# A routed encoder layer on one core: router products on rows before their norm, and the last expert's final tiles in five buffers

## The chip, the cores and the metric

The kernel runs on one core of one Trainium2 chip. The metric is the device time of one execution in microseconds. Engines are called PE (TensorE), VectorE (DVE), ScalarE (ACT), GpSimd (POOL) and SP (SyncE); SP, ScalarE and GpSimd also issue DMAs, each from a queue of its own.

## The reference, cut to what matters

One layer (DEPTH is 1) with the pooling mixer, then 16 experts that each choose 258 of the 2064 tokens, then a final norm. Everything is float32.

```python
D_MODEL, SEQ, N_META, N_EXPERTS, D_EXPERT = 1024, 2048, 16, 16, 2048
def _rmsnorm(x, g):
    return x * rsqrt(mean(x * x, axis=-1) + 1e-6) * g
h = concatenate([meta, x])                              # 2064 rows
u = _rmsnorm(h, norm_mix)
h = h + _pool_mixer(u, pool_w, pool_scale)              # window means, then a 256x256 map per group
u = _rmsnorm(h, norm_ffn)
aff = softmax(u @ router_w)                             # over the 16 experts
g, idx = top_k(aff.T, 258)                              # each expert picks its tokens
for e in range(16):
    xs = u[idx[e]]
    ys = (silu(xs @ w_gate[e]) * (xs @ w_up[e])) @ w_down[e] * g[e]
    h[idx[e]] += ys
out = _rmsnorm(h, norm_final)[16:]
```

A row's norm multiplies the whole row by one number and each column by its norm_ffn. So the logits of a row can also be had as (h @ (norm_ffn * router_w)) times that row's inverse root.

## The kernel before, in words

**Phase 1** works through 19 tiles of 128 rows (each shares 16 rows with its neighbour). The engines each run a written-out pipeline, `step(i0, j)`, in which `here(a)` stands for work on tile i0 + a: steps -1 to 2 are written out, 12 run in loops of four, the rest (up to step 21) is written out as the drain. For tile i:

- ScalarE squares the rows and takes the root (L839, L827), VectorE scales the band matrices by the inverse root (`make_band`, L1081), PE multiplies the rows by them (L1537, step i-1), ScalarE and VectorE split the result in a high and a low half (`pooled_hi` L855, `pooled_lo` L1099).
- PE's projection (24 matmuls, L1564, step i) gives the mixed rows, VectorE adds the input (`h_mid`, L1118), SP stores them to `h_acc` (L563).
- ScalarE squares `h_mid` and takes the root `rms2` (L864, L867, step i+1), VectorE multiplies by the inverse root and by norm_ffn (`u_out`, L1104 and L1109), SP stores it to `u_rows` (L567).
- PE transposes `u_out` (`turn_rows`, L1512 to L1521, at the end of step i+2), ScalarE copies the result to `u_t` (L874), PE multiplies it by the widened router matrix `rw_wide` (L1549, step i+3), VectorE copies the partial sums (`partial`, L1095), and a small matmul (the fold, L1568) adds them into the logits of that tile in PSUM.

PE's order within a step is: the bands' product of tile i0+1, the router's product of tile i0-3, the projection of tile i0, the fold of tile i0-3, the transposes of tile i0-2. The drain steps have the transposes first. In ScalarE's order the activation table for exp is loaded (L869) right behind the last root and ahead of the copy of `u_t`.

The start: SP issues all loads from one queue in a written order (L523 to L551). norm_mix comes as 8 rows (`nmix_rows`), which PE transposes to a column per block; VectorE scales the pooling weights `pw` by it as soon as they have landed (L1134).

**The routing** (L1170 to L1325) runs on VectorE, ScalarE and PE in a chain of short operations: softmax over all 19 tiles at once (L1174 to L1182), a digit-by-digit search for each expert's threshold in ten rounds, ranks, and the first expert's list. Its tables `tile_cum`, `rank`, `chosen` and `place` are used only there.

**The experts.** Each of the 16 has 48 quarters (32 of gate and up, 16 of down), 24 matmuls each in the last expert. ScalarE rounds a weight block to `w_hi` (L935), VectorE takes the rest `w_lo` (L1345), three blocks ahead of PE; a block of the ring of four is free when PE has finished the quarter four before. PE waits on `split_lo`. Each engine's order is written out by quarter.

**The last expert** also carries the final norm of all 2048 output rows, 16 tiles of 128 (`finals`, `square_final`, `store_final`, `reload_final`, `invert_final`, `final_tile`). Its steps are counted from quarter 8 on: step s is quarter s + 8, so steps 24 to 39 are the quarters 0 to 15 of the down projection. Tile t sits in buffer t % 3. At step 6 + 2t ScalarE squares it (L947), GpSimd adds eps and raises to -1/2 (L784, L788), VectorE multiplies by it and by norm_final (L1394). At step 7 + 2t ScalarE issues the store (it waits for VectorE), and in that step it also waits for the store of tile t - 1 to have landed and issues the load of tile t + 2 in its place. The first three loads are GpSimd's (L775). All of this is in the same in-order queues as `w_hi` and `w_lo`.

Tokens of the last expert are corrected behind it: `turn_last` transposes the results in four parts, VectorE adds them to the gathered rows (`add_last`, L1457), ScalarE squares them (`square_last`, L1016), VectorE multiplies by norm_final (`weigh_last`) and at last by the inverse root (L1476), GpSimd scatters them to the output (L817). Part 0 is added at quarters 9 to 11 of the down projection and squared ahead of the last `w_hi`; then come, on VectorE, part 1, the last final tile, the weighing of both parts, part 2.

## Time and profile before

| what | value |
|---|---|
| three timed runs | 2455.67 us median (2455.53 to 2458.54) |
| the profiled execution | 2459.78 us, span 2457.9 us, clock 0.984 |
| PE busy | 2386.1 us, 97% |
| PE's weight loads (PEld) | 2228.5 us, 91% |
| VectorE, ScalarE, GpSimd busy | 1865.9 us (76%), 1204.1 us (49%), 844.8 us (34%) |
| chain that ended last | PE 87%, issue 3%, VectorE 1%, GpSimd 1%, ScalarE 1% |
| one expert in the chain | 139.3 us from one to the next |

The durations of single operations come from the profiled execution. A matmul's duration in the trace is its latency; from one to the next it is about 0.12 us at the full clock. In the rows, "idle before <-releaser" is the time in which that engine did nothing ahead of the row, and who ended it. L1505 is the helper of all matmuls and L1510 that of all transposes, so they are told apart by their tiles. ScalarE's and SP's DMA issues (ACTq, SPq) take the queue's time though they are not counted as busy.

### The profile page before, as it was taken

How to read it: one execution, taken by the hardware profiler on the slowest of the kernel's cores; microseconds unless marked ns; L12 is line 12 of the kernel's file. 1: busy time of each engine (PE TensorE's matmuls, PEld its weight loads, DVE VectorE, ACT ScalarE, POOL GpSimd, SP SyncE). 2: the span in 40 equal slices, each digit the busy share in tenths (PEclk: the TensorE clock that was granted, in tenths of full speed). 3: DMA queues.
4: the chain of work that ended last, by engine and by line, in shares of the span. 5: the costliest groups of instructions: out<-in, count | busy, mean ns of one | idle time of the engine just before them, and what ended most of it. 6: DMA issues, size and time to landing. Idle time of an engine off the chain costs nothing.

```text
span 2457.9 us, 48606 instructions
## 1 busy us (share of the span) xinstructions
PE 2386.1 (97%) x17338; PEld 2228.5 (91%) x17338; DVE 1865.9 (76%) x2259; ACT 1204.1 (49%) x1938; POOL 844.8 (34%) x1013
## 2 busy tenths in 40 slices
PE   7958999999999999999999999999999999999997
PEld 7947989898999989899998989899998989899996
DVE  5666786869787786968788686968778686968765
ACT  5754444444544444454444444454444444454564
POOL 0001525234251524334251524335152533425111
PEclk9978999999999999999999999999999999999998
DMA  7764648486775858586774858586674948576594
GB/s 236 215 195 131 186 133 257 150 243 184 210 201 157 228 144 252 158 238 173 207 213 141 242 141 249 157 238 188 184 216 136 250 143 250 170 228 199 161 335 171
DMA packets 345810, 486.11 MB, mean 198 GB/s; under 512 B 23117, under 2 KB 294997, under 8 KB 345778
## 3 DMA queue, kind: packets, MB, share of 16 engines
q1 hardware_dynamic: 318370, 433.82, 59.2%
q0 software_dynamic: 23232, 36.67, 7.0%
q10 hardware_dynamic: 4176, 15.21, 1.6%
q8 instruction: 18, 0.29, 0.0%
q14 instruction: 14, 0.11, 0.0%
HBM read 443.27 MB, written 46.31 MB: 199 GB/s over the span
## 4 chain that ended last, share of the span: by engine, by line
PE 87%; issue 3%; DVE 1%; POOL 1%; ACT 1%; DMA 0%; DVEq 0%; POOLq 0%; ACTq 0%
PE bank L1505 86%; PE bank L1510 1%; ACT marks_a L913 0%; POOL fin L788 0%; DMA x_rows<-u_rows,idx 0%; DVE w_lo L1345 0%; POOL h_rows L796 0%; DVE h_rows L1466 0%; POOL fin L784 0%; POOL out L817 0%; DVE x_lo L1350 0%; DVE key_t L1226 0%; DVE y_rows L1457 0%; DVE marks_v L1200 0%; DVE flag L1207 0%
## 5 line engine op out<-in xcount | busy, mean ns | idle before, releaser
L1505 PE MATMUL bank<-x_lo,w_hi 128*128 128x258 f32 x4096 | 1157.6, 283 | 0.0
L1505 PE MATMUL bank<-x_hi,w_hi 128*128 128x258 f32 x4096 | 1156.5, 282 | 0.8 <-DVE w_lo L1345 0.7
L1505 PE MATMUL bank<-x_hi,w_lo 128*128 128x258 f32 x4096 | 1155.9, 282 | 0.0
L1345 DVE TENSOR_TENSOR w_lo<-raw,w_hi 128x1024 fp32r<-128x1024 f32 x584 | 713.8, 1223 | 114.0 <-ACT w_hi L935 109.7
L1505 PEld LDWEIGHTS bank<-x_hi,w_hi 128*128 128x128 f32 x4096 | 776.1, 189 | 14.7 <-issue 13.0
L1505 PEld LDWEIGHTS bank<-x_hi,w_lo 128*128 128x128 f32 x4096 | 777.6, 190 | 0.0
L1505 PEld LDWEIGHTS bank<-x_lo,w_hi 128*128 128x128 f32 x4096 | 776.9, 190 | 0.6
L935 ACT ACTIVATE w_hi<-raw 128x1024 fp32r<-128x1024 f32 x581 | 612.2, 1054 | 312.0 <-PE bank L1505 295.2
L671 POOL TENSOR_TENSOR carrier<-carrier 128x1 f32<-128x1 f32 x360 | 115.3, 320 | 1125.7 <-ACT y_rows L986 454.8
L716 POOL DMA_INDIRECT list_rows<-pair_now,slot_now x285 | 410.1, 1439 | 137.1 <-issue 137.1
L1371 DVE SCALAR_TENSOR_TENSOR acc_left<-raw,hid_left,acc_left 128x1024 f32<-128x1024 f32 x330 | 422.5, 1280 | 0.0
L1404 DVE TENSOR_TENSOR hid<-silu,bank 128x258 f32<-128x258 f32 x256 | 108.1, 422 | 329.4 <-PE bank L1505 329.4
L1505 PE MATMUL bank<-w_hi,hid_hi 128*128 128x512 f32 x960 | 304.5, 398 | 0.0
L1505 PE MATMUL bank<-w_lo,hid_hi 128*128 128x512 f32 x960 | 299.7, 393 | 0.0
L1505 PE MATMUL bank<-w_hi,hid_lo 128*128 128x512 f32 x960 | 299.2, 393 | 0.0
L1003 ACT ACTIVATE hid_left<-hid 128x2 f32<-128x2 f32 x244 | 49.7, 204 | 435.2 <-DVE hid L1404 435.2
L1345 DVE TENSOR_TENSOR w_lo<-raw_more,w_hi 128x1024 fp32r<-128x1024 f32 x184 | 224.8, 1222 | 40.2 <-ACT w_hi L935 38.4
L935 ACT ACTIVATE w_hi<-raw_more 128x1024 fp32r<-128x1024 f32 x184 | 193.7, 1053 | 101.8 <-PE bank L1505 101.8
L998 ACT ACTIVATE silu<-bank 128x258 f32<-128x258 f32 x256 | 99.0, 387 | 280.9 <-PE bank L1505 280.9
L1505 PEld LDWEIGHTS bank<-w_hi,hid_lo 128*128 128x128 f32 x960 | 180.6, 188 | 41.4
L1505 PEld LDWEIGHTS bank<-w_lo,hid_hi 128*128 128x128 f32 x960 | 180.4, 188 | 41.2
L1505 PEld LDWEIGHTS bank<-w_hi,hid_hi 128*128 128x128 f32 x960 | 175.1, 188 | 35.5
(209 smaller groups left out, 1887.9 us busy)
## 6 DMA issues: line engine op xcount, KB each, us to landing
raw<-in_moe_w_down SPq DMA_DIRECT2D x98, 1024.0 KB
raw<-in_moe_w_gate SPq DMA_DIRECT2D x97, 1024.0 KB
raw<-in_moe_w_up SPq DMA_DIRECT2D x97, 1024.0 KB
raw_more<-in_moe_w_gate SPq DMA_DIRECT2D x31, 1024.0 KB
raw_more<-in_moe_w_up SPq DMA_DIRECT2D x31, 1024.0 KB, 8.5
raw_more<-in_moe_w_down SPq DMA_DIRECT2D x30, 1024.0 KB, 6.5
h_in<-in_x SPq DMA_DIRECT2D x18, 512.0 KB, 5.6
h_acc<-h_mid SPq DMA_DIRECT2D x17, 448.0 KB, 4.9
```

What stands on the lines that cost most here:

```text
L671: nc.gpsimd.tensor_tensor(carrier[:, 0:1], carrier[:, 1:2], carrier[:, 1:2], ALU.mult)\
L716: pool.indirect_dma_start(list_rows, bass.IndirectOffsetOnAxis(ap=slot_now[:, c:c + 1], axis=0), pair_now[:, c, :], None, bounds_check=CAP ...
L935: nc.scalar.activation(w_hi[:, a % 4], split_view(a, last), ACT.Copy).then_inc(split_hi, 1)
L998: nc.scalar.activation(silu[:, fc], bank[:, q % 4, 0:CAP], ACT.Silu)\
L1003: nc.scalar.activation(hid_left[:, 4 * b + fc], hid[:, fc % 2, 256:CAP], ACT.Copy)\
L1345: nc.vector.tensor_tensor(w_lo[:, a % 4], split_view(a, last), w_hi[:, a % 4].bitcast(f32), ALU.subtract).then_inc(split_lo, 1)
L1371: nc.vector.scalar_tensor_tensor(out=acc_left[:, t], in0=down_row_view(k), scalar=by, in1=acc_left[:, t], op0=ALU.mult, op1=ALU.add)\
L1404: nc.vector.tensor_tensor(hid[:, fc % 2], silu[:, fc], bank[:, q % 4, 0:CAP], ALU.mult).then_inc(hid_done, 1)
L1505: return nc.tensor.matmul(dst, lhs, rhs, start=start, stop=stop)
L1510: return nc.tensor.matmul(dst, src, ident[0:n, 0:n], is_transpose=True, start=True, stop=True)
```

## The change

Part 1 (phase 1): PE transposes `h_mid` in place of `u_out`, one step earlier, and the router product and the fold follow one step earlier too. norm_ffn goes into the router's matrix: its 8 rows are loaded behind norm_mix's, transposed with them, and GpSimd multiplies where it copied. The roots of all tiles are kept in `rms2`, and the logits are multiplied by their inverse in the routing. `u_out` is still made and stored.

Part 2 (last expert): five buffers instead of three, the two new ones in the memory of the routing's tables, and a table of steps `FIN_AT` in place of every second step. A tile is stored two steps behind its square and its buffer reloaded four steps behind. In a step all stores and loads are issued ahead of the square. The gather of the last expert's rows on GpSimd stands behind tile 6 in place of tile 8 (both at step 22).

```diff
+FIN_RING = 5
+FIN_AT = (7, 9, 12, 14, 17, 19, 22, 24, 26, 28, 29, 31, 32, 34, 35, 36)
+FIN_EARLY = 7
@@ tiles
+        rms2 = sb("rms2", [P, NT], f32)
+        inv_all = sb("inv_all", [P, NT], f32)
+        counts = sb("counts", [P, 2 * D], f32)
+        tile_cum, rank = (counts[:, 2 * i * NE * NT:2 * (i + 1) * NE * NT].rearrange("p (k e c) -> p k e c", k=2, e=NE)
+                          for i in range(2))
+        chosen, place = (counts[:, i * NE * NT:(i + 1) * NE * NT].rearrange("p (e c) -> p e c", e=NE)
+                         for i in (4, 5))
-        fin_rows = [x_rows[:, 0], x_rows[:, 1], x_more[:]]
+        fin_rows = [x_rows[:, 0], x_rows[:, 1], x_more[:], counts[:, 0:D], counts[:, D:2 * D]]
@@ SP
-            sp.dma_start(nmix_rows[:], norm_mix[0].rearrange("(k p) -> k p", p=P)).then_inc(loaded_nmix, 16)
+            for i, rows in enumerate((norm_mix, norm_ffn)):
+                sp.dma_start(nmix_rows[KD * i:KD * (i + 1), :], rows[0].rearrange("(k p) -> k p", p=P))\
+                  .then_inc(loaded_nmix, 16)
@@ GpSimd
-            nc.gpsimd.tensor_copy(rw_wide[:, :, 0:NE], rw[:]).then_inc(rw_widened, 1)
+            pool.wait_ge(nmix_out, 1)
+            nffn_across = nmix[:, KD:2 * KD].unsqueeze(2).broadcast_to([P, KD, NE])
+            nc.gpsimd.tensor_tensor(rw_wide[:, :, 0:NE], rw[:], nffn_across, ALU.mult).then_inc(rw_widened, 1)
...
-            for s in range(3):
+            for s in range(FIN_RING):
                 pool.dma_start(fin_rows[s], h_acc[P * s + META:P * s + META + P, :]).then_inc(fin_first[s], 16)
...
-            for r in range(3):
-                for s in range(3):
-                    invert_final(3 * r + s, s, r)
+            for t in range(FIN_EARLY):
+                invert_final(t)
@@ ScalarE, step
-                    root(rms2[:, s:s + 1], ss2[:, s:s + 1], rooted2)
+                    root(rms2[:, column(i0, j, -1)], ss2[:, s:s + 1], rooted2)
...
-                if here(-2):
-                    act.wait_ge(turned, upto(i0, j, -2))
-                    if upto(i0, 0, -3) > 0:
-                        act.wait_ge(part_routed, upto(i0, j, -3))
+                if here(-1):
+                    act.wait_ge(turned, upto(i0, j, -1))
+                    if upto(i0, 0, -2) > 0:
+                        act.wait_ge(part_routed, upto(i0, j, -2))
                     nc.scalar.activation(u_t[:], two_banks(4), ACT.Copy).then_inc(turned_out, 1)
@@ ScalarE, last expert
-                t = (step_ - FIN_STEP) // 2
-                if step_ % 2 == 0 and 0 <= t < NFIN:
-                    square_final(t % 3, t // 3)
-                if step_ % 2 == 1 and 0 <= t < NFIN - 1:
-                    store_final(t, t % 3)
-                if step_ % 2 == 1 and 0 <= t - 1 < NFIN - 3:
-                    reload_final(t - 1, (t - 1) % 3, (t - 1) // 3)
-                if step_ == FIN_STEP + 2 * NFIN:
-                    store_final(NFIN - 1, (NFIN - 1) % 3)
+                for t, at in enumerate(FIN_AT):
+                    if step_ == at + 2:
+                        store_final(t, t % FIN_RING)
+                    if step_ == at + 4 and t + FIN_RING < NFIN:
+                        reload_final(t, t % FIN_RING, t // FIN_RING)
+                for t, at in enumerate(FIN_AT):
+                    if step_ == at:
+                        square_final(t % FIN_RING, t // FIN_RING)
@@ VectorE, step
-                if here(-3):
-                    s = (i0 - 3) % 2
-                    dve.wait_ge(part_routed, upto(i0, j, -3))
+                if here(-2):
+                    s = (i0 - 2) % 2
+                    dve.wait_ge(part_routed, upto(i0, j, -2))
...
                     nc.vector.tensor_copy(partial[:, s, :], bank[:, 7, s * P:(s + 1) * P]).then_inc(part_out, 1)
...
-                        dve.wait_ge(turned, upto(i0, j, -3))
...
                         dve.wait_ge(squared2, upto(i0, j, -2))
+                        dve.wait_ge(turned, upto(i0, j, -2))
@@ VectorE, routing
+            dve.wait_ge(rooted2, NT)
+            link(nc.vector.reciprocal(inv_all[:], rms2[:]))
             dve.wait_ge(routed, NT)
             logits = bank[:, 6, 0:NT * NE].rearrange("p (c e) -> p c e", e=NE)
-            link(nc.vector.tensor_reduce(peak[:], logits, AX.X, ALU.max))
-            nc.vector.tensor_tensor(lg[:], logits, over_experts(peak[:]), ALU.subtract).then_inc(shifted, 1)
+            link(nc.vector.tensor_tensor(lg[:], logits, over_experts(inv_all[:]), ALU.mult))
+            link(nc.vector.tensor_reduce(peak[:], lg[:], AX.X, ALU.max))
+            nc.vector.tensor_tensor(lg[:], lg[:], over_experts(peak[:]), ALU.subtract).then_inc(shifted, 1)
@@ VectorE, last expert (down projection)
-                if q % 2 == 0 and (24 + q - FIN_STEP) // 2 < NFIN - 1:
-                    final_tile((24 + q - FIN_STEP) // 2)
+                if 24 + q in FIN_AT[:-1]:
+                    final_tile(FIN_AT.index(24 + q))
@@ PE
-                s = (i0 - 2) % 2
-                pe.wait_ge(normed, upto(i0, j, -2))
-                if upto(i0, 0, -3) > 0:
-                    pe.wait_ge(turned_out, upto(i0, j, -3))
+                s = (i0 - 1) % 2
+                pe.wait_ge(mixed, upto(i0, j, -1))
+                if upto(i0, 0, -2) > 0:
+                    pe.wait_ge(turned_out, upto(i0, j, -2))
                 for k in range(KD):
                     last = turn_block(bank[:, 4 + k // 4, (k % 4) * P:(k % 4 + 1) * P],
-                                      u_out[:, s, k * P:(k + 1) * P])
+                                      h_mid[:, s, k * P:(k + 1) * P])
```

The rest of the diff moves the same offsets by one in the waits and loop ends of each engine (the router's product and fold from -3 to -2, the drain's last step from 21 to 20) and replaces 3 by FIN_RING in the semaphores and waits of the final tiles.

## Rows read from the trace of the kernel before

**Rows 1.** The page's 40 slices of 61.4 us: busy tenths of TensorE.

```profile
PE   7958999999999999999999999999999999999997
```

**Rows 2.** Stretches, 60 to 80 us: us, busy (instructions) by engine, clock, DMA, GB/s.

```profile
60.00:80.00 20.00, 19.87 (x199) 18.43 (x198) 13.29 (x21) 14.02 (x25) 0.00 (x0) 1.00 0.71 214
```

**Rows 3.** Timeline of TensorE, last expert: start, us, what, [idle before <-releaser].

```profile
2408.48 0.39 PE L1505 MATMUL bank<-hid_hi,w_hi 128*128 128x258 f32 x1 [0.64 <-DVE w_lo L1345]
...
2441.73 0.55 PE L1510 MATMUL bank<-ident,y_t 128*128 128x128 f32 x3 [1.64 <-ACT y_t L1042]
```

**Rows 4.** Timeline of TensorE in phase 1, step 17.

```profile
130.21 0.64 PE L1505 MATMUL bank<-u_t,rw_wide 128*32 128x128 f32 x16
...
130.78 0.38 PE L1505 MATMUL bank<-pw_hi,pooled_hi 128*128 128x256 f32 x1
...
133.84 1.07 PE L1510 MATMUL bank<-ident,u_out 128*128 128x128 f32 x8
```

**Rows 5.** Timeline of all engines, drain of phase 1 and start of the routing.

```profile
140.75 1.02 ACT L874 ACTIVATE u_t<-bank 128x1024 f32<-128x1024 f32 x1 [3.42 <-PE bank L1510]
...
142.92 0.64 PE L1505 MATMUL bank<-u_t,rw_wide 128*32 128x128 f32 x16
...
143.16 1.28 ACT L869 ACT_TABLE_LOAD   x1
...
143.63 0.29 DVE L1095 COPY partial<-bank 128x128 f32<-128x128 f32 x1 [2.69 <-PE bank L1505]
...
143.98 0.40 PE L1505 MATMUL bank<-cst,partial 128*128 128x16 f32 x2 [0.41 <-DVE partial L1095]
...
144.45 1.02 ACT L874 ACTIVATE u_t<-bank 128x1024 f32<-128x1024 f32 x1
...
148.74 1.08 PE L1505 MATMUL bank<-u_t,rw_wide 128*32 128x128 f32 x16 [0.18 <-ACT u_t L874]
...
150.95 0.47 DVE L1174 TENSOR_REDUCE peak<-bank 128x19 f32<-128x304 f32 x1 [0.63 <-PE bank L1505]
...
151.46 0.47 DVE L1175 TENSOR_TENSOR lg<-bank,peak 128x304 f32<-128x304 f32 x1
```

**Rows 6.** Timeline of all engines, fill of phase 1 (steps 2 and 3).

```profile
29.49 0.36 PE L1505 MATMUL bank<-pw_hi,pooled_hi 128*128 128x256 f32 x1 [0.64 <-DVE h_mid L1118]
...
30.88 1.06 ACT L839 ACTIVATE squares<-h_in 128x1024 f32<-128x1024 f32 x1 [4.19 <-DMA h_in<-in_x]
...
33.30 1.22 DVE L1099 TENSOR_TENSOR pooled_lo<-bank,pooled_hi 128x1024 fp32r<-128x1024 f32 x1 [0.22 <-ACT pooled_hi L855]
...
34.58 2.05 PE L1505 MATMUL bank<-band,h_in 128*128 128x128 f32 x16 [1.18 <-DVE pooled_lo L1099]
```

**Rows 7.** Stretches of TensorE: us, busy (instructions), granted clock, DMA, GB/s.

```profile
146.00:147.00 1.00, 1.00 (x19) 0.91 0.67 174
...
208.00:210.00 2.00, 2.00 (x18) 0.93 0.00 0
```

**Rows 8.** Timeline of the start: SyncE's issue of norm_mix, VectorE's scaling.

```profile
2.58 0.38 SPq L532 DMA_DIRECT2D nmix_rows<-in_norm_mix  x1
...
11.71 1.67 DVE L1134 SCALAR_TENSOR_TENSOR pw<-pw,nmix,pscale 128x256 f32<-128x256 f32 x4 [2.19 <-DMA pw<-in_pool_w]
```

**Rows 9.** Timeline of ScalarE, VectorE and TensorE, end of the last expert.

```profile
2425.75 1.05 ACT L947 ACTIVATE junk<-x_more 128x1024 f32<-128x1024 f32 x1
...
2427.82 1.29 DVE L1394 SCALAR_TENSOR_TENSOR x_more<-x_more,fin,nfin 128x1024 f32<-128x1024 f32 x1 [0.97 <-POOL fin L788]
...
2429.68 1.22 DVE L1345 TENSOR_TENSOR w_lo<-raw,w_hi 128x1024 fp32r<-128x1024 f32 x1
...
2430.03 0.82 PE L1510 MATMUL bank<-ident,y_t 128*128 128x128 f32 x6
...
2432.21 1.04 ACT L935 ACTIVATE w_hi<-raw 128x1024 fp32r<-128x1024 f32 x1
...
2435.60 1.26 DVE L1394 SCALAR_TENSOR_TENSOR x_rows<-x_rows,fin,nfin 128x1024 f32<-128x1024 f32 x1
```

More of the change, by code:

```diff
@@ L798, in _ @@
                     .then_inc(last_gathered, 16)
-            for r in range(3, NFIN // 3):
-                for s in range(3):
-                    invert_final(3 * r + s, s, r)
-            for t in range(NFIN // 3 * 3, NFIN):
-                invert_final(t, t % 3, t // 3)
+            for t in range(FIN_EARLY, NFIN):
+                invert_final(t)
             pool.wait_ge(last_squared, 6)
@@ L811, in _ @@
             nc.gpsimd.tensor_tensor(early_ss[:, 2], part_ss[:, 2], early_ss[:, 1], ALU.add).then_inc(early_summed, 1)
-            for s in range(3):
-                pool.wait_ge(fin_stored[s], 16 * len(range(s, NFIN, 3)))
+            for s in range(FIN_RING):
+                pool.wait_ge(fin_stored[s], 16 * len(range(s, NFIN, FIN_RING)))
             pool.wait_ge(last_placed, 2)
@@ L885, in _ @@
                     step(FIRST + r, j)
-            for i in range(FIRST + BODY * TURNS, NT + 2):
+            for i in range(FIRST + BODY * TURNS, NT + 1):
                 step(i, 0)
@@ L1103, in step @@
                     dve.wait_ge(rooted2, upto(i0, j, -1))
-                    nc.vector.reciprocal(inv2[:, s:s + 1], rms2[:, s:s + 1]).then_inc(inverted2, 1)
+                    nc.vector.reciprocal(inv2[:, s:s + 1], rms2[:, column(i0, j, -1)]).then_inc(inverted2, 1)
                     dve.wait_ge(inverted2, upto(i0, j, -1))
                     if upto(i0, 0, -3) > 0:
-                        dve.wait_ge(turned, upto(i0, j, -3))
                         dve.wait_ge(stored_u[s % 2], 16 * (turn(i0, j, -1, 2) - 1))
@@ L1151, in _ @@
                     step(FIRST + r, j)
-            for i in range(FIRST + BODY * TURNS, NT + 3):
+            for i in range(FIRST + BODY * TURNS, NT + 2):
                 step(i, 0)
@@ L1527, in step @@
                 tail = isinstance(j, int) and i0 >= NT
-                if tail and here(-2):
+                if tail and here(-1):
                     turn_rows(i0, j)
@@ L1565, in step @@
                     last.then_inc(projected, 1)
-                if here(-3):
-                    pe.wait_ge(part_out, upto(i0, j, -3))
-                    mm(bank[:, 6, ds(NE * (i0 - 3) + (BODY * NE) * j, NE)], partial[:, (i0 - 3) % 2, :],
+                if here(-2):
+                    pe.wait_ge(part_out, upto(i0, j, -2))
+                    mm(bank[:, 6, ds(NE * (i0 - 2) + (BODY * NE) * j, NE)], partial[:, (i0 - 2) % 2, :],
                        const("fold"), True, True).then_inc(routed, 1)
-                if here(-2) and not tail:
+                if here(-1) and not tail:
                     turn_rows(i0, j)
-            pe.wait_ge(loaded_nmix, 32)
-            turn_block(bank[:, 7, 0:KD], nmix_rows[:]).then_inc(nmix_turned, 1)
+            pe.wait_ge(loaded_nmix, 48)
+            turn_block(bank[:, 7, 0:2 * KD], nmix_rows[:]).then_inc(nmix_turned, 1)
             for i in range(-1, FIRST):
@@ L1583, in _ @@
                     step(FIRST + r, j)
-            for i in range(FIRST + BODY * TURNS, NT + 3):
+            for i in range(FIRST + BODY * TURNS, NT + 2):
                 step(i, 0)
```

58 lines of the change are left out of this document (29 added, 29 removed).

## The prediction

> **What bounds the kernel now.** I read the page first: in 40 slices of 61 us TensorE (PE) is busy nine tenths or more in all but the first four and the last [rows 1]. The sixteen experts are PE's own time, and nothing in the change touches PE's work there. So I looked only at three places: the fill and drain of phase 1 (0 to 151 us), the routing behind it (151 to 214 us, short dependent VectorE and ScalarE operations), and the last expert with its end (2302 us on). A microsecond won ahead of 214 us is handed on by the experts as it is; one lost there too.
>
> In the steady part of phase 1 PE is busy 19.87 of 20 us with 199 matmul records, and a tile has 66 of them (16 for the bands, 16 for the router, 24 for the projection, 2 for the fold, 8 transposes): 6.6 us a tile, while VectorE is busy 13.3 and ScalarE 14.0 of the 20 [rows 2]. PE waits for nobody there, so the others have room. In the last expert PE stands still twice only, 0.64 and 1.64 us [rows 3].
>
> The sums stand against the profiled execution, 2459.78 us (its span is 2457.9). The median of the three timed runs is 2455.67, 4.1 us less; I carry the difference over to the median unchanged. 0.2% is 4.9 us, about what a measurement of this kernel can tell from no change.
>
> **Part 1, the drain of phase 1.** The transposes now read h_mid, so square, root, reciprocal and norm leave the path of a tile, and the lag falls from two steps to one. PE does the same work, but of the three tiles' worth that stood behind the last projection one goes in front of it: the transposes (1.07 us), the router product (0.57, from 130.21 to 130.78) [rows 4] and its fold of two short matmuls, 0.40 us when it stands alone [rows 5] and less in a full queue: 1.8 us. Where PE is the bound, that would move the last projection back by 1.8 us. It comes in at the fill, in steps 1 and 2, and there PE idles: 0.64 us for h_mid and 1.18 us for pooled_lo [rows 6], together 1.82. The second wait goes back to ScalarE, which sat 4.19 us until the load of tile 4 had landed at 30.88 [rows 6]; a busier PE doesn't move that. What the earlier router adds to this chain is VectorE's copy of partial (0.29 us by [rows 5]) ahead of pooled_lo at 33.30, where VectorE has 0.22 us of idle time [rows 6]. I take +0.1; bounds 0 and +1.8.
>
> Then the drain. Before, the ScalarE copies of the transposed rows start at 140.75 (tile 16), 144.45 (tile 17) and, behind another transpose, about 147.7 (tile 18); the router product of tile 18 starts at 148.74 and the routing's first VectorE operation at 150.95 [rows 5]. After, the copy at 140.75 is tile 17's, and that at 144.45, held there by the activation table load of 143.16, is tile 18's. It ends at 145.47; the transposes of tile 18 need only h_mid (done 140.94, about) and run in the slot of 141.92. So the last router product starts at 145.5 instead of 148.74. From there to the routing's first operation it took 2.21 us before, at the half clock. Tile 16's product of 142.92 was followed by its fold at 143.98 at the full clock [rows 5], 1.06 against 1.49 us. The granted clock is 1.00 until 146 and 0.91 in 146 to 147 [rows 7], so most of it is at the full clock (2.4 GHz): I take 1.65 us, 147.15 instead of 150.95, or -3.8. Bounds: -3.3 (2.21 us again) and -3.9.
>
> Added behind it: one multiplication of the 304 logits by the inverse roots, from PSUM. The nearest row is the subtraction, the same shape from the same bank, 0.47 us, and it starts 0.51 us after the reduction ahead of it [rows 5]; +0.5, with bounds 0.4 and 0.7. The reciprocal of all 19 roots costs some 0.3 us, but lies between the last copy of partial and the last fold, where VectorE waits anyway; if that cover is gone it costs at most that 0.3. The reduction and the subtraction now read SBUF, at no gain I can see.
>
> The Trainium skill ("ScalarE: Activation LUTs", section "What ACT_TABLE_LOAD costs") gives a table load about 2.66 us, of which 1.38 us is a drain behind the 1.28. The trace does not agree here: the copy of 144.45 starts 1.29 us after the load. By the page the last copy would end 1.4 us later and this part would give 1.4 us less.
>
> **Part 1, the start.** SP issues one DMA more, ahead of the load of tile 1: each such issue takes about 0.4 us [rows 8]. What sets the start is the landing of pw's first half, for which VectorE waited 2.19 us until 11.71 [rows 8]; it is the last of some 2.5 MB, and I take it to be limited by bandwidth. +0.2, bounds 0 and 0.4. GpSimd's widening multiplies instead of copying, off the path: PE needs it only at about 30 us, it is issued at 23. The transposition of 16 rows instead of 8 and its copy of 16 columns hide behind the first band. The column of rms2 written by a register costs nothing I can see; ScalarE and VectorE have 6 us of 20 free in phase 1 [rows 2].
>
> Part 1 in sum: -3.8 + 0.5 + 0.1 + 0.2 = **-3.0 us**.
>
> **Part 2, the last expert.** With five buffers ScalarE stores a tile two steps after its square instead of one, and the tile it reloads is needed 3 to 8 steps later instead of 3. ScalarE's waits at a store (for VectorE's product) and at a load go; the waits for a store to have landed keep their distance of two steps. PE's stall of 0.64 us before 2408.48 [rows 3] comes from such waits: w_hi late, the final tile late, w_lo behind it on VectorE. I expect it to go, and PE to be 0.8 us ahead from there (0.64 and a slow first matmul).
>
> What is late next is the end, and there the new rhythm is denser: tiles 12 to 15 at steps 32, 34, 35, 36, where it was 30, 32, 34, 36. So VectorE has one final tile more between add_last(0) and add_last(2). The walk: quarter 12 of the down projection ended at 2430.03 [rows 9], now 2429.2, so quarter 10, two quarters of 2.87 us before, at 2423.5. ScalarE copies y_t, issues a store (0.38) and squares tile 13 from 2424.4. The product of a tile starts 2.07 us after its square (2425.75 to 2427.82): 2426.5. Then VectorE, in order: that product and add_last(1) 1.86 (2427.82 to 2429.68), w_lo 1.2, the product of tile 14 1.2, add_last(2) 0.7 [rows 9], which is 2431.4. ScalarE squares that part and starts the last w_hi at 2432.1; before it was 2432.21 [rows 9]. One store is issued ahead of the square of tile 15 (+0.38), so that its product starts at 2435.55; before 2435.60 [rows 9]. From there the order is the old one: the copies of y_t, the transposes, the wait of 1.64 us, the end. PE's 0.8 us are lost again in front of the last transposes. **Sum 0 us**; bounds -1.0 (the end follows PE, and a little of the 1.64 goes too) and +1.2 (the 0.64 stays, and the end is 0.4 late).
>
> Moved past: GpSimd issues five first loads instead of three, 1.2 us of issue more, 12 us before anybody needs it. The final stores of tiles 13 and 14 come later, but tile 15's, the last, where it was, and the last scatter waits for VectorE. The gather of h_rows stays at step 22.
>
> **The rivals.**
> A (0.14): the cover of part 1 is thinner than it looks. If the fill does not take the 1.8 us in, 1.7 us of the gain go. Time 2455.67 - 1.3 = 2454.4. For it: PE is the bound from step 3 on. Against it: the idle time is there and is set by a DMA.
> B (0.16): the end follows PE. Then part 2 gives its 0.8 and up to 1.2 of the 1.64 us: 2455.67 - 3.0 - 2.0 = 2450.7. For it: PE really does wait at the end. Against it: VectorE's backlog sets that wait, and the new rhythm adds to it.
> C (0.07), slower: PE's clock returns later. Everything from 151 us on moves by 3 us against whatever decides the clock. Before, it was back at 0.93 in 208 to 210 [rows 7], as the first expert began. Each microsecond in which it is back later costs half of one; from 6.0 us of lateness the change is slower than before, and at 8 us it is 2456.7. Against it: the pattern of work ahead of 208 is the same. The Trainium skill ("TensorE: Matmul & The Clock Gate", Part 1) says that the point at which the clock changes varies from run to run, by about half a microsecond, which would be 0.25 us here.
> D (0.06): the shorter lag doesn't shorten anything, since the last logits wait for VectorE's u_out of tile 18 (144.0 to 145.3), queued ahead of the last partial. Then only the start is paid: 2455.9. Against it: it ends before the last router product does.
>
> **How the numbers follow.** My forecast (0.57) is 2455.67 - 3.0 = **2452.7**. Its own bounds are -3.9+0.4-1.0 = -4.5 and about -1.0. The range takes in B and A and most of C: 2449.9 to 2456.3. Faster by over 4.9 us: B's better half and a little of the forecast's edge, 0.15. Slower by over 4.9: 0.04, C and what I have not seen. Within: 0.81.
>
> **What would show it.** In the new trace: last router product at about 145.5 to 146 (with the shift of the start), the reduction's new multiplication near 147.5, the experts' first matmuls some 3 us earlier; PE without the idle 1.18 us at the fill; no stall at quarter 6 of the down projection; a wait of 1 us before the transposes inside the last quarter; the last final tile at its place relative to the end. Wrong, if the last projection is more than 0.5 us late, if the distance from 151 us to the experts changes, or if the last expert is over 1 us shorter or longer.

## The result and the profile after

The changed kernel takes **2461.34 us** (median of 22 runs, 2459.0 to 2463.74) against 2457.43 us before (22 runs, 2454.7 to 2460.32) in the same comparison: ratio 1.0018, interval 1.0012 to 1.0024. It is 3.9 us slower where 3.0 us faster was forecast, outside the range, and the interval excludes no change. The profiled execution took 2459.57 us, its span is 2457.6; that of before was 2459.78, so the two profiles by themselves show no loss. Single executions of one kernel differ by 5 us here, so I compare stretches inside the profiles and medians between kernels. The forecast stood on a median of three runs, 2455.67; over 22 runs the same kernel has 2457.43. Of the 8.6 us between forecast and result (2452.7 and 2461.34) that is 1.8; the change itself is off by 6.9.

The page of the changed kernel, busy times and PE's 40 slices, answers to [rows 1]: it differs by one tenth in three slices (the first, the third and the last).

```profile
PE 2385.9 (97%) x17338; PEld 2229.0 (91%) x17338; DVE 1865.9 (76%) x2261; ACT 1205.0 (49%) x1938; POOL 850.9 (35%) x1015
...
PE   8948999999999999999999999999999999999996
```

**The drain of phase 1** [rows 5]. Timeline of ScalarE, PE and VectorE in the changed kernel, 141 to 148 us:

```profile
141.88 1.28 ACT L879 ACT_TABLE_LOAD   x1
143.18 1.02 ACT L884 ACTIVATE u_t<-bank 128x1024 f32<-128x1024 f32 x1
...
144.25 0.72 PE L1519 MATMUL bank<-u_t,rw_wide 128*32 128x128 f32 x16 [1.16 <-ACT u_t L884]
...
146.09 0.47 DVE L1187 TENSOR_TENSOR lg<-bank,inv_all 128x304 f32<-128x304 f32 x1 [0.33 <-PE bank L1519]
146.60 0.47 DVE L1188 TENSOR_REDUCE peak<-lg 128x19 f32<-128x304 f32 x1
```

From the table load to the first operation of the routing it is 4.21 us (141.88 to 146.09) instead of 7.79 (143.16 to 150.95), and the multiplication adds 0.51 (146.09 to 146.60): the drain gives what was forecast.

**The fill** [rows 6]: the square of tile 4 and the band products of tiles 2 and 4.

```profile
29.52 1.06 ACT L849 ACTIVATE squares<-h_in 128x1024 f32<-128x1024 f32 x1 [1.33 <-DMA h_in<-in_x]
...
21.51 1.95 PE L1519 MATMUL bank<-band,h_in 128*128 128x128 f32 x16
...
33.38 1.95 PE L1519 MATMUL bank<-band,h_in 128*128 128x128 f32 x16
```

PE's idle 0.64 and 1.18 us are gone, and VectorE no longer idles ahead of pooled_lo.

**The last expert** [rows 3]: every wait of PE in the timeline from 2300 us on.

```profile
2405.39 0.39 PE L1519 MATMUL bank<-hid_hi,w_hi 128*128 128x258 f32 x1 [2.15 <-DVE w_lo L1359]
...
2433.85 0.39 PE L1519 MATMUL bank<-hid_hi,w_hi 128*128 128x258 f32 x1 [0.27 <-DVE w_lo L1359]
...
2437.02 0.55 PE L1524 MATMUL bank<-ident,y_t 128*128 128x128 f32 x3 [1.82 <-ACT y_t L1053]
...
2441.03 0.90 PE L1524 MATMUL bank<-ident,y_t 128*128 128x128 f32 x3 [1.00 <-ACT y_t L1053]
```

Here the time is. I measure the last expert from PE's first transposition of its gathered rows (2268.67 here) to the last transposes of y_t (2441.03): 172.36 us, against 168.46 before (2273.27 to 2441.73). From there to the end of the span it is 16.6 and 16.2 us. PE now waits 5.2 us in it instead of 2.3, which is 3.0 of the 3.9 us that the last expert grew. The stall that I expected to go (0.64) has grown to 2.15. Another 0.65 us come with PE's clock. In these stretches (PE's busy time, granted clock, DMA share, GB/s), the changed kernel first and the kernel before second, it is at 0.61 instead of 1.00:

```profile
2438.00:2440.00 2.00, 2.00 (x12) 0.61 0.15 59
```

```profile
2438.00:2440.00 2.00, 2.00 (x18) 1.00 0.50 205
```

Ahead of it PE had waited 1.82 us. From those transposes to the last ones it is 4.01 us here and 4.00 before, although the wait inside is 1.00 instead of 1.64: the matmuls between take 3.01 us instead of 2.36. The last 0.2 us I didn't trace.

ScalarE is what is late, and the summary of its waits from 2335 to 2458 us (us in total, times, longest) says for what:

```profile
ACT junk L959 <- DMA out<-x_rows: 5.8, 1, 5.8
...
ACT junk L959 <- DMA out<-counts: 3.2, 1, 3.2
...
ACT junk L959 <- DMA out<-x_more: 2.5, 1, 2.5
ACT w_hi L945 <- DMA out<-x_rows: 2.4, 1, 2.4
...
ACT w_hi L945 <- DMA out<-counts: 2.1, 2, 1.4
```

With a last 0.4 us these are 16.4 us of waiting until a final store has landed, a wait that was 4.4 us before. ScalarE's timeline shows how it comes about:

```profile
2388.92 0.35 ACTq L949 DMA_DIRECT2D x_rows<-h_acc  x1
...
2389.42 0.34 ACTq L964 DMA_DIRECT2D out<-x_rows  x1
...
2399.88 0.35 ACTq L949 DMA_DIRECT2D x_rows<-h_acc  x1
2400.27 0.44 ACTq L964 DMA_DIRECT2D out<-x_more  x1
2400.84 1.06 ACT L959 ACTIVATE junk<-counts 128x1024 f32<-128x1024 f32 x1 [5.78 <-DMA out<-x_rows]
```

At 2388.92 a reload is issued and half a microsecond later a store of the same size behind it on the same queue. The next reload needs that store landed and is issued only at 2399.88: 10.5 us after the store. ScalarE, which also makes w_hi and y_t, stands in that wait for 5.78 us. Then it is late and comes to the next such waits nearer in time to their stores. The next store, at 2400.27, stands behind that wait too, where in the kernel before a step's store was issued ahead of its wait.

### The profile page after: what moved, and what is told of

The parts are those of the page before. It is cut to its first block, busy times and chain, and to the rows that moved or that the text cites. A ratio compares the mean times of both kernels' runs of the same rounds, so it can differ in the third digit from the quotient of the medians.

```text
span 2457.6 us, 48640 instructions
## 1 busy us (share of the span) xinstructions
PE 2385.9 (97%) x17338; PEld 2229.0 (91%) x17338; DVE 1865.9 (76%) x2261; ACT 1205.0 (49%) x1938; POOL 850.9 (35%) x1015
## 4 chain that ended last, share of the span: by engine, by line
PE 87%; issue 2%; DVE 1%; DMA 1%; ACT 1%; POOL 1%; ACTq 0%; DVEq 0%; POOLq 0%
PE bank L1519 86%; PE bank L1524 1%; ACT marks_a L923 0%; DMA out<-x_rows 0%; POOL fin L802 0%; DMA x_rows<-u_rows,idx 0%; DMA out<-x_more 0%; POOL fin L798 0%; DVE h_rows L1480 0%; POOL out L827 0%; ACT junk L959 0%; DVE key_t L1240 0%; DVE counts L1408 0%; DVE w_lo L1359 0%; DVE y_rows L1471 0%
```

## The experiments

Medians of 11 runs each (5 for `load_ahead` and `old_rhythm`), against runs of the kernel before on the same chip, in three groups whose medians of before were 2457.2 (first four kernels), 2456.93 (next four) and 2456.62 (last four). "Waits for stores" is ScalarE's from 2335 to 2458 us.

| kernel | median us | ratio to before, interval | last expert us | waits for stores us |
|---|---|---|---|---|
| part1 | 2455.94 | 0.9996 (0.9987 to 1.0005) | 168.96 | 7.7 |
| part2 | 2462.16 | 1.0020 (1.0011 to 1.0029) | 171.00 | 11.9 |
| stores_first | 2457.15 | 1.0002 (0.9993 to 1.0011) | 168.50 | 6.7 |
| reload_late | 2456.97 | 0.9999 (0.9990 to 1.0008) | 168.44 | 0 |
| load_ahead | 2466.76 | 1.0039 (1.0026 to 1.0053) | 178.02 | 17.9 |
| old_rhythm | 2468.93 | 1.0051 (1.0037 to 1.0064) | 179.45 | 19.2 |
| end_early | 2454.20 | 0.9989 (0.9980 to 0.9998) | 166.37 | 3.2 |
| fill_twice | 2458.14 | 1.0004 (0.9995 to 1.0013) | 170.15 | 3.4 |
| rows_by_act | 2453.95 | 0.9990 (0.9981 to 0.9999) | 166.18 | 3.3 |
| extra_row | 2458.10 | 1.0003 (0.9994 to 1.0012) | 167.49 | 3.8 |
| end_early_old | 2456.65 | 0.9998 (0.9989 to 1.0007) | 166.11 | 2.6 |
| fill_twice_new | 2457.98 | 1.0006 (0.9997 to 1.0015) | 168.69 | 3.0 |

The column of the last expert is from one profile per kernel. Before, `extra_row` and `fill_twice` have the same code there and show 168.46, 167.49 and 170.15 us, so a difference of 1 to 2 us in that column says nothing by itself.

### Each part alone

`part1` is the kernel before with the transposes of h_mid and the roots on the logits; `part2` the kernel before with the five buffers and the new rhythm.

> Part 1 alone (router products on rows not yet normed); the last expert as before. Two traces show the first expert's steady state some 4.6 us earlier with the change, of which I had forecast 3.0. Theory: this part wins by itself, 2.5 to 5 us: ratio 0.9980 to 0.9990. Rival: part of what the profile shows at the start is chance of that execution, and the ratio is 0.9990 to 1.0000. Last expert in the trace as before: PE stall of about 0.64 us at quarter 6 of the down projection.

> Part 2 alone (five buffers, new rhythm); phase 1 as before. Theory: this part loses all that the changed kernel lost and what part 1 won, 6 to 9 us: ratio 1.0025 to 1.0037. In the trace ScalarE waits over 15 us in all at reloads for stores to land. Rival: part 1 is worth nothing in the median and this part loses about 4 us, ratio 1.0016.

The loss is part 2's: +5.0 us in the median, its last expert 171.00 us. That is between the 6 to 9 us of the theory and the 4 of the rival, and ScalarE's waits are 11.9 us where over 15 were expected. Part 1 gains 1.3 us in the median; its ratio lies in the rival's range and not in the theory's, but its interval takes in 1 as well as the theory's nearer end.

### The two ways to mend the store

`stores_first` and `reload_late` are the changed kernel with one edit each.

```
 stores_first
                 for t, at in enumerate(FIN_AT):
                     if step_ == at + 2:
                         store_final(t, t % FIN_RING)
+                for t, at in enumerate(FIN_AT):
                     if step_ == at + 4 and t + FIN_RING < NFIN:
 reload_late
-                    if step_ == at + 4 and t + FIN_RING < NFIN:
+                    if t + FIN_RING < NFIN and step_ == min(at + 6, FIN_AT[t + FIN_RING] - 2):
```

> The changed kernel with one exchange: in a step of the last expert all stores are issued ahead of the loads (before: the older tile's reload, then the younger tile's store behind it in the same queue). Theory Q (queue order): the 512 KB load in front makes the store land later, and the reload two steps on waits for it; then out-stores land in 4 to 5 us instead of 6, ScalarE's waits at reloads fall from about 18 us to under 6, and the ratio falls from 1.0018 to 0.998 to 0.9995. Theory D (distance): stores land late anyway, since the weights fill the DMA engines; ratio stays 1.001 to 1.002. Theory R (dense rhythm at the end): ratio stays 1.001 to 1.002 and the end of the trace doesn't move.

> The changed kernel, but a buffer is reloaded up to six steps behind its square instead of four (no later than two steps ahead of its next square); the order of loads and stores within a step is left as changed. Theory D: what costs is that ScalarE waits only two steps behind the store; ratio 0.998 to 0.9995. Theory Q alone: the landing times of stores stay at 6 us, but four steps of distance cover them too, so the ratio falls as well, while the landing times tell the two apart. Theory R (dense rhythm): ratio stays at 1.001 to 1.002.

Either edit takes the loss against the kernel before away: 168.50 and 168.44 us for the last expert, some 4.3 us off the median of the changed kernel. Against part 1 alone (2455.94 in the same comparison) 1.0 to 1.2 us are left, too little to tell from nothing, and the ratios are above the 0.998 to 0.9995 that the theories gave. In `stores_first` the reload waits for its store two steps on as in the change, and only the order inside a step is another: two steps are enough if the store of a step comes first, so theory D as it was written falls, and Q stands. `reload_late` shows that the distance alone is a cure as well. Its stores still land late (5.9, 5.6 and 5.4 us in the median of the three tiles, 6.1, 6.0 and 5.4 in the changed kernel), and the one in the place of 2389.42 took 9.2 us, but nobody waits two steps behind them:

```profile
out<-x_rows ACTq DMA_DIRECT2D x1, 512.0 KB, 9.2
```

So the loss takes both, the new order and a wait only two steps behind the store. With the waits gone PE's stall is too, and what is left is what the walk of the prediction had. PE's waits in `reload_late` from 2300 us on:

```profile
2434.54 0.55 PE L1524 MATMUL bank<-ident,y_t 128*128 128x128 f32 x3 [0.94 <-ACT y_t L1053]
...
2438.55 0.55 PE L1524 MATMUL bank<-ident,y_t 128*128 128x128 f32 x3 [1.64 <-ACT y_t L1053]
```

### The order alone, and the rhythm alone

`load_ahead` puts the suspected order into the kernel before; `old_rhythm` takes the new rhythm out of the changed kernel and leaves the order.

```
 load_ahead (on the kernel before)
-                if step_ % 2 == 1 and 0 <= t < NFIN - 1:
-                    store_final(t, t % 3)
                 if step_ % 2 == 1 and 0 <= t - 1 < NFIN - 3:
                     reload_final(t - 1, (t - 1) % 3, (t - 1) // 3)
+                if step_ % 2 == 1 and 0 <= t < NFIN - 1:
+                    store_final(t, t % 3)
 old_rhythm (on the changed kernel)
-FIN_AT = (7, 9, 12, 14, 17, 19, 22, 24, 26, 28, 29, 31, 32, 34, 35, 36)
-FIN_EARLY = 7
+FIN_AT = tuple(range(6, 38, 2))
+FIN_EARLY = 9
```

> The kernel before, three buffers and its old rhythm, with one edit: at every odd step ScalarE issues the reload ahead of the store instead of behind it. Theory Q (a store queued behind a 512 KB load on ScalarE's queue lands so late that the wait for it, two steps on, holds ScalarE): the stores land 5 to 7 us after their issue instead of 3.5 to 4.2, ScalarE's waits at stores in the last expert rise from 4.4 us to over 10, the last expert (168.46 us before) is 2 to 4 us longer, the time +2 to +4 us. Rival (it takes the five buffers or the dense rhythm; the order alone does nothing): last expert within 0.5 us of 168.46, time within 1 us of before.

> The changed kernel with the old rhythm of squares (steps 6, 8, ... 36) and the gather behind tile 8 again; five buffers, store two steps on, reload four steps on, the reload of a step ahead of its store, as the change has them. With a square in every second step, each step with a reload has a store behind it. Theory Q: last expert 171 to 173 us as in the changed kernel (172.36), time some 4 us over the kernels that have the store first (2457.2), so about 2461. Rival R (the dense rhythm at the end makes ScalarE late, and the old one would not): last expert 168.5, time about 2456.5.

Two swapped lines in the kernel before cost 9.6 us in the last expert and 9.8 in the median. The direction is theory Q's, the size over twice the most that it gave (2 to 4 us). The landings, in the summary of DMA issues from 2335 to 2440 us (last column: median us from issue to landing), first of the kernel before, then of `load_ahead`:

```profile
out<-x_rows ACTq DMA_DIRECT2D x11, 512.0 KB, 4.2
...
out<-x_more ACTq DMA_DIRECT2D x5, 512.0 KB, 3.5
```

```profile
out<-x_rows ACTq DMA_DIRECT2D x10, 512.0 KB, 6.0
...
out<-x_more ACTq DMA_DIRECT2D x5, 512.0 KB, 6.8
```

The medians hide where this happens. Store by store, after 2405 us a store lands in 2.6 to 3.4 us before and, behind a load, in 5.3 to 5.8 in `load_ahead`. From 2364 to 2401 us it is 5.5 to 7.5 us before, with no load ahead, and 6.3 to 9.5 in `load_ahead`. The means there are 6.6 and 7.0 us, so in that stretch the queue makes little of the difference. But there the second thing that the swap does counts: with the reload first, the wait for the older store stands ahead of the issue of the younger one. Each reload in `load_ahead` but the first leaves within 0.1 us of its store's landing and the next store 0.4 to 1.1 us behind it, so every landing over two steps (5.7 us) moves all that follows; before, the younger store had left already. The swap makes both changes at once, and no run separates them: how much of the 9.6 us is the queue and how much the place of the wait is open.

ScalarE's waits and PE's in `load_ahead`:

```profile
ACT w_hi L935 <- DMA out<-x_more: 13.2, 4, 5.4
...
ACT w_hi L935 <- DMA out<-x_rows: 4.7, 2, 3.3
```

```profile
PE bank L1505 <- DVE w_lo L1345: 4.4, 6, 2.1
PE bank L1510 <- ACT y_t L1042: 3.2, 3, 1.6
```

`old_rhythm` refutes the rival that the dense end makes the loss: with an even rhythm it is 7 us more (179.45), where the theory had 171 to 173. Two of PE's waits and the stretches behind them show why it is so much:

```profile
2385.91 0.58 PE L1519 MATMUL bank<-x_hi,w_hi 128*128 128x258 f32 x1 [3.25 <-DVE w_lo L1359]
...
2414.97 0.39 PE L1519 MATMUL bank<-hid_hi,w_hi 128*128 128x258 f32 x1 [3.40 <-DVE w_lo L1359]
```

```profile
2386.00:2388.00 2.00, 2.00 (x9) 0.50 0.27 37
...
2416.00:2418.00 2.00, 2.00 (x11) 0.50 0.86 217
```

PE waits 9.1 us in all, 6.8 more than before; behind each of the two long waits its granted clock is at 0.50 for some microseconds, and that is about the remaining 4.2 of the 11.0 us. (Estimated from windows of 2 us: it is below 1.00 from 2384 to 2392 and from 2414 to 2420, and PE's busy time there, times what the clock lacks, is 4.4 us.)

A reload at +4 and a store at +2 fall into one step whenever two squares stand two steps apart. In the old rhythm that is so in all 11 steps with a reload, in the new one in 7 (11, 16, 21, 26, 28, 30, 33). The uneven rhythm spares the changed kernel part of the loss.

### A rhythm that ends earlier

```
 end_early (on reload_late)
-FIN_AT = (7, 9, 12, 14, 17, 19, 22, 24, 26, 28, 29, 31, 32, 34, 35, 36)
-FIN_EARLY = 7
+FIN_AT = (6, 8, 10, 12, 14, 16, 18, 20, 22, 24, 26, 27, 29, 30, 31, 33)
+FIN_EARLY = 9
-                    ... step_ == min(at + 6, FIN_AT[t + FIN_RING] - 2):
+                    ... step_ == min(at + 6, FIN_AT[t + FIN_RING] - 3):
-                if 24 + q in FIN_AT[:-1]:
+                if 24 + q in FIN_AT:
-            final_tile(NFIN - 1)
```

> The changed kernel with the reloads late (min of 6 steps after the square and 3 steps ahead of the next square in the buffer), and squares at steps 6, 8, ... 24, 26, 27, 29, 30, 31, 33 instead of a last one at 36: the last final tile is out of VectorE's queue before add_last(1). Theory (the end is set by VectorE's and ScalarE's backlog, not by PE): the wait of 1.64 us before the last transposes and the one of about 1 us ahead of them shrink, together by 1.2 to 2.2 us, so the last expert takes 166.3 to 167.3 us instead of 168.5, and the time is about 2455 (1.5 to 2 us under the late reload alone, 2456.97). Rival (the last down quarters have the copies and the transposes in a chain of their own, whatever VectorE does beside them): last expert 168.3 to 168.7, time about 2457.

2454.20 us, 7.1 under the changed kernel and faster than the kernel before by an interval that excludes 1. The last expert takes 166.37 us. VectorE's timeline has the last product of a final tile in front of the first add_last, where the changed kernel has three behind it, and PE has one wait left:

```profile
2420.70 1.28 DVE L1408 SCALAR_TENSOR_TENSOR x_rows<-x_rows,fin,nfin 128x1024 f32<-128x1024 f32 x1 [0.71 <-POOL fin L802]
2421.90 0.75 DVE L1471 SCALAR_TENSOR_TENSOR y_rows<-bank,gates,h_rows 128x512 f32<-128x512 f32 x1
```

```profile
2436.77 0.55 PE L1523 MATMUL bank<-ident,y_t 128*128 128x128 f32 x3 [0.47 <-ACT y_t L1053]
```

In this kernel the reloads are ahead of the stores of their steps as in the change, and its stores land in 5.7 to 6.5 us in the median, but mostly four steps lie between store and wait, and ScalarE waits only 3.2 us. The gain took the earlier end together with the late reload; whether three buffers could carry such an end wasn't tried. The mechanism of rival B was there (the end can follow PE), only not in this rhythm.

### How much idle time the fill has

`fill_twice` issues the 16 band products of tile 3 twice in the kernel before, `fill_twice_new` the same in `part1`: 1.7 us more for PE, the values the same.

```
+                    for again in range(2 if i0 == 2 and isinstance(j, int) else 1):
                         for k in range(KD):
                             ...
                             last = mm(bank[:, k // 4, ...
```

> The kernel before with the 16 band products of tile 3 issued twice in the fill of phase 1 (1.7 us more for PE, the same result): is there idle time of PE in the fill that takes 1.8 us in, as the prediction has it? Theory F (only some 0.9 us: what PE idled in the profile of before was long because that execution's load of tile 4 landed late, 6.7 us after its issue; in an execution of the same phase 1 with 5.2 us there was less): from the product of tile 2 to that of tile 4 it takes about 11.8 us against 10.95 in such an execution, if the load lands fast, and 12.3, hidden, if it takes 6.7 us; the time +0.3 to +0.9 us. The prediction's own view: 12.26 as before at either landing, time as before. If the load were not in it at all: 12.65, time +1.7.

> Part 1 alone with the band products of tile 3 issued twice in the fill. All six profiles with part 1 have 11.87 to 11.93 us from the product of tile 2 to that of tile 4 whether its load took 5.2 or 6.2 us; PE would be the bound there and no cover left. Theory F: 13.5 to 13.6 us (the whole 1.71 us comes on top), the time +1.7 over part 1 alone, about 2457.6. Rival (cover is left, since the load of tile 4 sets it): under 13, time +0 to +1.

Band products of tiles 2 and 4 in `part2`, whose phase 1 is that of before, and of tiles 2, 3 and 4 in `fill_twice` and in `fill_twice_new`:

```profile
21.78 1.95 PE L1506 MATMUL bank<-band,h_in 128*128 128x128 f32 x16
...
32.73 1.95 PE L1506 MATMUL bank<-band,h_in 128*128 128x128 f32 x16
```

```profile
21.73 1.95 PE L1505 MATMUL bank<-band,h_in 128*128 128x128 f32 x16
...
26.31 3.73 PE L1505 MATMUL bank<-band,h_in 128*128 128x128 f32 x32
...
33.59 1.95 PE L1505 MATMUL bank<-band,h_in 128*128 128x128 f32 x16
```

```profile
22.62 1.95 PE L1518 MATMUL bank<-band,h_in 128*128 128x128 f32 x16
...
28.09 3.74 PE L1518 MATMUL bank<-band,h_in 128*128 128x128 f32 x32
...
36.28 0.94 PE L1518 MATMUL bank<-band,h_in 128*128 128x128 f32 x7
```

From tile 2 to tile 4: 10.95, 11.86 and 13.66 us. Of the 1.7 us added, the old fill hides 0.8 and the new one nothing, as theory F had it. The medians went up by 1.2 us over the kernel before in `fill_twice` and, by the ratios, by some 2.4 over part 1 alone in `fill_twice_new` (expected 0.3 to 0.9 and 1.7), which their intervals of 2 to 3 us do not tell from the expected. The old fill has 10.92 to 10.96 us in three profiles (`part2`, `load_ahead`, `end_early_old`; tile 4's load lands 5.1 to 5.2 us after its issue) and 12.26 and 12.30 in two (before, `extra_row`; 6.7 us). The new one has 11.87 to 11.93 in six, and 12.01 in `rows_by_act`, with that load landing in 5.4 to 6.4 us. The profile that the prediction read was one of the two with the late load: the new fill costs 0.9 us against the usual old one.

### The start, and what part 1 is worth

`extra_row` is the kernel before with SP loading norm_ffn's row too, unused. `rows_by_act` is `end_early` with both rows loaded by ScalarE's queue. `end_early_old` is `end_early` without part 1.

```
 rows_by_act: the two loads leave SP's block and open ScalarE's
+            for i, rows in enumerate((norm_mix, norm_ffn)):
+                act.dma_start(nmix_rows[KD * i:KD * (i + 1), :], rows[0].rearrange("(k p) -> k p", p=P))\
+                   .then_inc(loaded_nmix, 16)
             nc.scalar.preload_act_table(ACT.Sqrt)
```

> The kernel before with one DMA more: SP loads the row of norm_ffn beside that of norm_mix, and nobody uses it. The start alone. Theory I: pw's first half in at 12.3 to 12.5 us, tile 1's product at 15.3, the time +0.5 us, too little for the median but readable in the profile. As predicted (+0.2): pw in at about 12.05. Rival B: pw in at 11.86 on average, time as before. One execution scatters by 0.4 us, so the issue times are read too: the loads of pw issued 0.35 us later.

> The kernel with the early end (end_early, 2454.2 us) with one edit: ScalarE's queue, idle at the start, issues the loads of the two norm rows, so that SP issues neither and everything behind them leaves 0.7 us earlier. In the six profiles with part 1 so far pw's first half is in at 12.42 us on average (11.80 to 13.01) and tile 1's band product starts at 15.37; in the four without it at 11.86 and 14.81. Theory I (the start follows SP's issue): pw in at 11.6 to 12.0, tile 1's product at about 14.6, the time 0.5 to 1 us under end_early, some 2453.5. Rival B (bandwidth sets it, and the queue that issues a row is of no matter): pw in at 12.4, the time as end_early's within 0.3 us.

> The final tiles of end_early (five buffers, late reloads, last square at step 33) on the phase 1 of the kernel before: a third pair that gives what part 1 is worth (the others are part 1 alone against before, -1.3 us, and the changed kernel against part 2 alone, -0.8 us). If the steps read from the traces hold (drain -3.65, multiplication +0.51, fill +0.93, start +0.5), this kernel is 1.7 us slower than end_early: about 2455.9. If part 1 is worth the predicted 3.0 us, about 2457.2; if nothing, 2454.2. Its last expert takes 166.4 us as end_early's.

The start can't be read this finely. pw is in at 12.68 us in `extra_row`, past theory I's 12.3 to 12.5, and at 12.77 in `rows_by_act`, where I forecast 11.6 to 12.0 and bandwidth 12.4; its ratio is `end_early`'s (0.9990 and 0.9989). So theory I in its form with SP's issue isn't borne out. Without the row pw came in at 11.33 to 12.48 (five profiles, mean 11.98), with it at 11.80 to 13.01 (nine, mean 12.46). What the row costs lies between nothing and 0.7 us, and I leave it there.

Part 1 is worth, by the three pairs of ratios, 1.0 us (0.9996), 0.5 (1.0018 against 1.0020) and 2.2 (0.9989 against 0.9998): 1.2 us on average, each with an interval of some 2 to 3 us on either side. The third pair lies between the 1.7 us that the steps gave and the predicted 3.0 and decides neither. Its steps in the profiles sum to more. From the table load to the first operation of the routing it is 7.97 us on average in the six profiles with the old drain and 4.13 in the eight with the new one, so -3.8, +0.5 for the multiplication, +0.9 for the fill and 0 to +0.7 for the start: -2.4 to -1.7. The profiles have one more measure of it, the start of the last expert: 2269.5 us on average in the six with part 1 and nothing else changed ahead of it, 2272.4 in the four without (before, `part2`, `load_ahead`, `end_early_old`), so -2.9. All of this fits within the intervals of the medians; what part 1 is worth is known no better than 1 to 3 us.

## Why the prediction was wrong, step by step

- **Drain, -3.8 (bounds -3.3 to -3.9): right.** From the table load on, 7.79 to 4.21 us is -3.6 in this pair of profiles, -3.8 on average. The chain was as walked: the copy behind the table load 1.30 us after it (143.18 - 141.88), the router product 2.4 us after the load, 1.84 us from there to the routing where I took 1.65.
- **Multiplication, +0.5: right** (0.51).
- **Fill, +0.1: mis-sized, it is +0.9**, inside its bounds. "It comes in at the fill, in steps 1 and 2, and there PE idles: 0.64 us for h_mid and 1.18 us for pooled_lo, together 1.82." The first is there in all five profiles with the old fill and nothing added to it (0.61 to 0.64), the second only in an execution in which tile 4's load is late; the row was no property of the kernel. Rival A, at half its price.
- **Start, +0.2:** not contradicted, open between 0 and 0.7.
- **Part 1 in sum, -3.0:** about -1.2 by the medians, -1.7 to -2.4 by the steps, -2.9 by the start of the last expert. Of what is missing only the fill's 0.8 is traced to a step.
- **Part 2, 0 in sum: this is the step that failed**, and of it one clause: "the waits for a store to have landed keep their distance of two steps". They do, in steps. But the loops of the change put the reload of a step ahead of its store, both on ScalarE's queue, where before the store came first. I costed this edit at nothing and didn't ask what the store now stands behind: a load of 512 KB in the queue, and in ScalarE's program the wait for the older store. `load_ahead` shows what the order costs by itself (9.6 us in the last expert), `stores_first` that without it the loss against before is gone; ScalarE's waits for stores, 4.4 us before, were 16.4 in the changed kernel and 6.7 in `stores_first`. With it fell "I expect it to go" of the 0.64 us stall, which became 2.15.
- **The rest of part 2: right.** Without the waits the stall goes, and PE's lead is lost again: 0.94 and 1.64 us of waiting at the last two transposes of `reload_late`, and its last expert is 168.44 us against 168.46 before. The prediction named "a wait of 1 us before the transposes inside the last quarter" and a sum of 0.
- **The clock (rival C): it did return later, and the price was wrong.** The first expert starts earlier, so it is the distance from its first matmul that counts. That matmul, the stretch in which PE's granted clock rises (the number ahead of the last two, 1.00 being 2.4 GHz), and PE's next wait, before:

```profile
207.10 0.55 PE L1505 MATMUL bank<-x_hi,w_hi 128*128 128x258 f32 x1
...
208.00:209.00 1.00, 1.00 (x9) 0.87 0.00 0
...
214.34 0.39 PE L1505 MATMUL bank<-x_hi,w_hi 128*128 128x258 f32 x1 [0.74 <-DVE w_lo L1345]
```

and in the changed kernel, which has no wait of PE in its first expert:

```profile
202.19 0.55 PE L1519 MATMUL bank<-x_hi,w_hi 128*128 128x258 f32 x1
...
206.00:207.00 1.00, 1.00 (x9) 0.94 0.62 104
```

The matmuls reach their short duration (0.28 us) 1.2 us behind the first one before and 4.0 us in the changed kernel. At half of each microsecond that would be 1.4 us, but from the first matmul of the first expert to that of the second it is 139.73 us before and 139.95 after: what an early clock gains, PE gives back in its wait for w_lo. In the five profiles in which the clock was back within 1.9 us of the first matmul PE waits 0.46 to 0.84 us there, in the nine in which it took 3.5 to 4.4 us it doesn't wait, and the distance between the experts is 139.72 to 140.12 us in all. At the drain the lower clock also comes earlier than in [rows 7], but PE has no matmul in that microsecond:

```profile
146.00:147.00 1.00, 0.00 (x0) 0.00 (x0) 0.88 (x2) 0.00 (x0) 0.00 (x0) 0.50 0.71 181
```

- **The rule on table loads** (the Trainium skill, "ScalarE: Activation LUTs", "What ACT_TABLE_LOAD costs"): the measurement decides against the 1.38 us of drain here as it did before; the copy starts 1.30 us after the load's start, and the load itself 0.02 us after the end of the root ahead of it.
- **The range** had a mechanism for "slower" (the clock) and none on ScalarE's queue. Its upper end was also added up too tightly: the worst bounds of the terms (-3.3, +0.7, +1.8, +0.4, +1.2) sum to +0.8 and not to about -1.0. The measured +3.9 lies outside of that sum too. What would have shown it was in the code and in the rows: a store and a load of 512 KB each, issued in one step, and a wait of ScalarE's own on the store.

## What to carry to other kernels

Where an engine itself waits for a store that it issued, write down what stands ahead of that store, in the queue and in the engine's program, not only how many steps lie between issue and wait; two lines in another order cost 10 us here. A buffer's reload belongs behind the stores of its step, or late enough that nobody waits for the landing, and the five buffers paid here only with a rhythm that also ends early enough that the last tiles are out of the way of the end. An idle time that a DMA's landing made in one profiled execution is no cover to count on.

## What the runs showed of the hardware

- A 512 KB store on ScalarE's queue landed in 2.6 to 3.4 us in the kernel before, after 2405 us, and, with a 512 KB load issued 0.4 us ahead of it, in 5.3 to 5.8 in `load_ahead`. From 2364 to 2401 us it took 5.5 to 7.5 us with no load ahead, though in `extra_row`, the same code, only 3.9 to 4.3 up to 2393; that of 2389.42 in the changed kernel, behind a load, took 10.4.
- The waits of the issuing engine feed on themselves, since an engine that is late has less time between its store and its wait: 1.8 to 3.3 us more per landing in the median, together with a wait that stands ahead of the next store, became 9.6 us in `load_ahead`.
- TensorE's granted clock fell to 0.50 behind waits of 3.25 and 3.40 us in `old_rhythm` and behind the 1.82 at the end of the changed kernel, and stayed at 1.00 behind the 2.15 at 2405.39. So a wait can cost more than its length, but not every one does.
- The same fill takes 10.9 or 12.3 us, as tile 4's load lands in 5.2 or 6.7. In both of the late executions of the old fill TensorE's granted clock had been 0.50 from 14 to 20 us, as in this window of `extra_row`; in the three others it was 0.72 or 1.00. But `fill_twice_new` was at 0.50 too, and its load landed in 5.6 us. Whether one has to do with the other wasn't tried.

```profile
14.00:20.00 6.00, 4.29 (x18) 4.02 (x19) 5.83 (x10) 3.93 (x6) 0.00 (x0) 0.50 1.03 323
```

- With the old rhythm and three buffers PE's stall in the middle of the last expert is 0 (`extra_row`), 0.41 (`part1`), 0.64 (before), 0.78 (`fill_twice_new`) or 1.41 us (`fill_twice`), in code that is the same there; a stall of one profile is a draw from these. In `extra_row` the stores landed early, as said above, and PE had no stall.
